# A 19-stage network on one core: the delta rule in 64-row blocks, weight splits placed anew, 512-column projection steps

## What is computed

```python
gc = jnp.cumsum(g, axis=-1)
decay = jnp.exp(jnp.where(causal, gc[..., :, None] - gc[..., None, :], -jnp.inf))
A = jnp.where(strict, jnp.einsum('bhncd,bhned->bhnce', k_beta, k) * decay, 0.0)
u = triangular_solve(eye + A, v * beta[..., None])
w = triangular_solve(eye + A, k_beta * jnp.exp(gc)[..., None])
attn_intra = jnp.where(causal, jnp.einsum('bhncd,bhned->bhnce', q, k) * decay, 0.0)
# for each of the four chunks in turn:
v_new = u_c - w_c @ state
o = qd @ state + a_c @ v_new
state = state * gl + kd.T @ v_new
```

## Time and profile before

| | |
|---|---|
| median of three runs | 3740.81 us (3738.6 to 3742.23) |
| the profiled execution's own time | 3740.95 us |
| its span in the profile | 3739.2 us |
| PE busy | 3435.3 us, 92% |
| DVE, ACT, POOL busy | 2060.6, 1559.5, 53.4 us |
| mean granted clock of TensorE | 0.943 |

### The profile page before, as it was taken

How to read it: one execution, slowest core, us unless ns; L and a number is a source line. 1 busy time by engine, 2 the same in 40 slices (tenths; PEclk the granted TensorE clock), 3 DMA queues, 4 the chain that set the end, 5 groups by cost and what they waited for, 6 DMA issues and landing times.

```text
span 3739.2 us, 48611 instructions
## 1 busy us (share of the span) xinstructions
PE 3435.3 (92%) x18972; PEld 2979.5 (80%) x18972; DVE 2060.6 (55%) x2413; ACT 1559.5 (42%) x1797; POOL 53.4 (1%) x84
## 2 busy tenths in 40 slices
PE   8986998998999999879999999999689999998899
PEld 6885887887887889768888888888668888887787
DVE  4557555545545567565554655555665455665554
ACT  4446444444444455114444444444344444531243
POOL 0000000000000020000000000000000000000000
PEclk9997998999999999789999999999889999988899
DMA  6542454454355554004555445555304555430154
GB/s 209 187 112 60 145 191 152 146 184 161 107 186 167 186 170 150 10 1 155 185 177 191 164 160 188 175 190 161 126 1 155 186 176 190 149 113 1 35 181 145
DMA packets 441172, 535.36 MB, mean 143 GB/s; under 512 B 21122, under 2 KB 405614, under 8 KB 441040
## 3 DMA queue, kind: packets, MB, share of 16 engines
q1 hardware_dynamic: 439248, 528.76, 44.1%
q0 software_dynamic: 1792, 4.72, 0.5%
HBM read 532.36 MB, written 1.05 MB: 143 GB/s over the span
## 4 chain that ended last, share of the span: by engine, by line
PE 86%; DVE 9%; ACT 3%; issue 1%; DMA 0%; SPq 0%; ACTq 0%; DVEq 0%
PE bank L132 22%; PE bank L134 22%; PE bank L133 22%; PE bank L129 3%; PE bank L130 3%; PE bank L131 3%; PE bank L309 2%; DVE w_lo L113 1%; PE bank L244 1%; ACT w_hi L105 1%; PE bank L1551 1%; PE bank L1558 1%; PE bank L1500 1%; PE bank L1581 1%; DVE arena L1750 1%
## 5 line engine op out<-in xcount | busy, mean ns | idle before, releaser
L113 DVE TENSOR_TENSOR w_lo<-raw,w_hi 128x2048 fp32r<-128x2048 f32 x514 | 1176.4, 2291 | 704.9 <-ACT w_hi L105 704.9
L105 ACT ACTIVATE w_hi<-raw 128x2048 fp32r<-128x2048 f32 x514 | 982.7, 1914 | 641.2 <-PE bank L134 527.4
L132 PE MATMUL bank<-w_hi,xT_hi 128*128 128x512 f32 (+3 forms) x3008 | 1101.9, 366 | 76.2 <-issue 33.2
L134 PE MATMUL bank<-w_hi,xT_lo 128*128 128x512 f32 (+3 forms) x3008 | 1088.4, 362 | 0.0
L133 PE MATMUL bank<-w_lo,xT_hi 128*128 128x512 f32 (+3 forms) x3008 | 1086.3, 361 | 0.0
L132 PEld LDWEIGHTS bank<-w_hi,xT_hi 128*128 128x128 f32 (+1 forms) x3008 | 580.0, 193 | 160.4 <-issue 43.5
L134 PEld LDWEIGHTS bank<-w_hi,xT_lo 128*128 128x128 f32 (+1 forms) x3008 | 578.7, 192 | 85.3
L133 PEld LDWEIGHTS bank<-w_lo,xT_hi 128*128 128x128 f32 (+1 forms) x3008 | 580.3, 193 | 79.8
L132 PE MATMUL bank<-w_hi,hidT_hi 128*128 128x512 f32 x1056 | 412.0, 390 | 0.0
L134 PE MATMUL bank<-w_hi,hidT_lo 128*128 128x512 f32 x1056 | 411.0, 389 | 0.0
L133 PE MATMUL bank<-w_lo,hidT_hi 128*128 128x512 f32 x1056 | 410.9, 389 | 0.0
(11 more groups left out here) (397 smaller groups left out, 2744.8 us busy)
## 6 DMA issues: line engine op xcount, KB each, us to landing
raw<-ffn_w_gate_up SPq DMA_DIRECT2D x352, 512.0 KB
raw<-ffn_w_down SPq DMA_DIRECT2D x264, 512.0 KB
raw<-ffn_w_gate SPq DMA_DIRECT2D x88, 512.0 KB
raw<-ffn_w_up SPq DMA_DIRECT2D x88, 512.0 KB
raw<-gdn_w_in SPq DMA_DIRECT2D x64, 512.0 KB
raw<-sc_w_in SPq DMA_DIRECT2D x24, 512.0 KB
raw<-rg_w_in SPq DMA_DIRECT2D x32, 336.0 KB
raw<-nsa_w_in SPq DMA_DIRECT2D x20, 512.0 KB
```

What stands on the lines that cost most here:

```text
L105: c.nc.scalar.activation(c.w_hi[r][:], c.raw[r][:], ACT.Copy).then_inc(c.sem("w_hi_split"), 1)
L113: c.nc.vector.tensor_tensor(c.w_lo[r][:], c.raw[r][:], c.w_hi[r][:].bitcast(F32), ALU.subtract).then_inc(c.sem("w_lo_split"), 1)
L132: mm(out, x_hi, w_hi, start=start, stop=False)
L134: return mm(out, x_lo, w_hi, start=False, stop=stop)
```

## The change

Three edits:

- **Delta rule.** Both chunks of a tile are kept in a 128 x 64 block, one chunk in rows 0 to 63, the other in rows 64 to 127, and all 16 pairs of head and tile (32 blocks of 64 x 64) go through together, in two groups of 8 (four heads, both tiles). Products are 64 x 64 x 64, ordered so that chunks, and thus row and column halves of the array, alternate (`quads`). q and k aren't scaled; the factors go into the small scalars. Preparation stands between gate steps. Masking of levels 2 to 5, the scalings of v and k and the gate's product move to POOL. In the recurrence the first chunk needs no state. ACT scales the state and reads `q state`. The output norm alternates between ACT, DVE and POOL.
- **Splits.** At the end of an FFN the split of slab b+3 moves ahead of the last hidden copy, and that of slab b+4 moves behind the next stage's norm (`late_slabs`: two slabs there instead of one, also after a stage whose last step has two slabs).
- **512-column steps.** Six groups of "tok" projections (the value half of w_kv, attn_w_o, sc_w_out, nsa_w_in, nsa_w_out, gdn_w_out twice) use steps of 512 columns, two slabs and two banks: 34 steps become 17.

```diff
+    for n in st.late_slabs:
+        dve_split(c, dve, slab_number(n, 0))
...
         hidden(f0 + j)
+        dve_split(c, dve, slab_number(b + 3, j))
         if last:
             last_hidden_lo(f0 + j)
-        dve_split(c, dve, slab_number(b + 3, j))
-        dve_split(c, dve, slab_number(b + 4, j))
+        else:
+            dve_split(c, dve, slab_number(b + 4, j))
...
+    def wide(weights, col0, steps):
+        return P_(weights, col0, steps, "tok", width=512, slabs=2, two_banks=True)
...
+def quads():
+    for flip in range(2):
+        for h4 in range(4):
+            for ch in range(2):
+                yield ch ^ flip, ch, h4
...
+    def small_products(b, lo, pair, lhs, rhs):
+        for t, ch, h4 in quads():
+            z, r = 8 * b + 4 * t + h4, rows_of(ch)
+            last = mm(c.bank[2 * pair + t][r, lo + h4 * G_CHUNK:lo + (h4 + 1) * G_CHUNK], lhs(r, z), rhs(r, z),
                       start=True, stop=True)
+        return last
...
+    for m in range(1, len(LEVELS)):
+        Am = v.Am[(m - 1) % 2]
+        for b in range(2):
...
+                pe.wait_ge(c.sem("gdn_X"), 8 * u + 2 * (m - 2) + b + 1)
+                pe.wait_ge(c.sem("gdn_A_level"), 10 * u + 2 * (m - 2) + 2 * (m > 3) + b + 1)
+            small_products(b, 0, b, lambda r, z: Am[r, z, :], lambda r, z: v.X[r, z, :]).then_inc(c.sem("gdn_ax"), 1)
+        for b in range(2):
+            pe.wait_ge(c.sem("gdn_T"), 12 * u + 2 * m + b + 1)
+            small_products(b, 256, b, lambda r, z: v.T[r, z, :], lambda r, z: v.Y[r, z, :]).then_inc(c.sem("gdn_y"), 1)
+            if m < len(LEVELS) - 1:
+                small_products(b, 0, 2 + b, lambda r, z: v.Y[r, z, :], lambda r, z: v.T[r, z, :]
+                               ).then_inc(c.sem("gdn_x"), 1)
...
+    pool.wait_ge(c.sem("gdn_tokens_read"), 2 * u + 1)
+    for b in range(2):
+        vb = by_tile(group(v.vb, b))
+        g.tensor_tensor(out=vb, in0=vb, in1=spread(group_cols(v.norm[:, :, G_HEADS:], b), G_DIM), op=ALU.mult
+                        ).then_inc(c.sem("gdn_tokens_scaled"), 1)
...
+    def level(m):
+        for b in range(2):
...
+            g.tensor_tensor(out=group(v.Am[(m - 1) % 2], b), in0=group(v.AQ, b)[:, :, 1, :],
+                            in1=per_head(v.level[m], 8), op=ALU.mult).then_inc(c.sem("gdn_A_level"), 1)
+    level(2)
+    level(3)
+    for b in range(2):
+        attn = group(v.AQ, b)[:, :, 0, :]
+        g.tensor_tensor(out=attn, in0=attn, in1=per_head(v.inclusive, 8), op=ALU.mult).then_inc(c.sem("gdn_A_level"), 1)
+    level(4)
+    level(5)
...
+    decay_state(1)
+    from_state(0)
+    decay_state(2)
+    squares(0)
+    root(0)
+    from_state(1)
+    squares(1)
+    root(1)
...
+    new_state(0)
+    new_values(1)
+    new_state(1)
+    new_values(2)
+    outputs(0)
+    new_state(2)
+    mean_squares(0)
+    new_values(3)
+    gated(0)
+    outputs(1)
+    mean_squares(1)
+    gated(1)
```

More of the change, by code:

```diff
@@ L585, in one @@
                 pe.wait_ge(c.sem("w_lo_split"), n + 1)
[L586 removed]
+        kd = pr.kd
+        kt = kd * len(slabs)
         lo, hi = pr.cols
@@ L589, in one @@
         if pr.two_banks:
-            order = [(tile, k) for q in range(len(slabs)) for tile in range(tiles) for k in range(q * KD, (q + 1) * KD)]
+            order = [(tile, k) for q in range(len(slabs)) for tile in range(tiles) for k in range(q * kd, (q + 1) * kd)]
         else:
@@ L1468, in pool_gdn @@
+    for m in range(len(LEVELS)):
+        step(g.tensor_tensor(out=v.full[m], in0=v.full[m], in1=v.upper, op=ALU.mult))
+    step(g.tensor_scalar(v.full[0], v.full[0], -1.0, None, ALU.mult))
+    compact = [(v.level[m], v.full[m]) for m in range(6)] + [(v.inclusive, v.upper), (v.ident, c.ident[:])]
+    for dst, src in compact:
+        for ch in range(2):
+            rows = slice(G_CHUNK * ch, G_CHUNK * (ch + 1))
+            step(g.tensor_copy(dst[rows, :], src[rows, rows]))
     assert made[0] == GDN_MASK_STEPS
-GDN_MASK_STEPS = 3 * 7 + 1 + 5 + 1 + 1
@@ L1598, in pe_gdn @@
-    pe_to_operand(c, pe, st, c.mix_out, "gdn_out", 2 * u + 2)
+    pe_project(c, pe, gate, after=beside_gate)
+    pe.wait_ge(c.sem("gdn_tokens_read"), 2 * u + 2)
+    for b in range(2):
+        for t in range(TOKS):
+            for h4 in range(4):
+                h = 4 * b + h4
+                for ch in range(2):
+                    tok = chunk_of(t, ch)
+                    last = mm(c.bank[4 + 2 * b + t][rows_of(ch), h4 * P:(h4 + 1) * P], v.cv[:, 8 + h, tok],
+                              v.cv[:, h:h + 9:8, tok], start=True, stop=True)
+            last.then_inc(c.sem("gdn_products"), 1)
@@ new lines, in pe_gdn @@
+    pe.wait_ge(c.sem("gdn_gaps"), 2 * u + 2)
+    pe.wait_ge(c.sem("gdn_kd_scale"), 2 * u + 2)
+    mm(c.bank[3][:, 0:2 * G_MATS], c.ones[0:G_MATS, :], flat(v.last), start=True, stop=True
+       ).then_inc(c.sem("gdn_products"), 1)
+    pe.wait_ge(c.sem("projection_read"), gate.step + gate.steps)
+    def small_products(b, lo, pair, lhs, rhs):
+        for t, ch, h4 in quads():
+            z, r = 8 * b + 4 * t + h4, rows_of(ch)
+            last = mm(c.bank[2 * pair + t][r, lo + h4 * G_CHUNK:lo + (h4 + 1) * G_CHUNK], lhs(r, z), rhs(r, z),
+                      start=True, stop=True)
+        return last
@@ new lines, in act_gdn, with decay_state @@
+    for b in range(2):
+        act.wait_ge(c.sem("gdn_uw"), 4 * u + b + 1)
+        if b == 0:
+            act.wait_ge(c.sem("gdn_y"), 10 * u + 10)
+        scalar.activation(flat(group(v.u, b)), c.pairs[b][:], ACT.Copy).then_inc(c.sem("gdn_u_read"), 1)
+    def decay_state(x):
+        act.wait_ge(c.sem("gdn_state"), 6 * u + 2 * (x - 1) + 2)
+        for h in range(G_HEADS):
+            n = x // 2 * G_HEADS + h
+            last = scalar.activation(v.decayed[:, h, :], v.state[:, h, :], ACT.Copy, scale=v.elast[:, x % 2, n:n + 1])
+        last.then_inc(c.sem("gdn_state_decayed"), 1)
```

724 lines of the change are left out of this document (398 added, 326 removed).

## The result

The changed kernel takes **3507.48 us** (median of 4 runs, 3506.62 to 3508.96) where the kernel before took 3739.7 beside it: ratio 0.938, interval 0.936 to 0.940, so 232 us less. The forecast was 3581, and even its range ended at 3530: right in sign, 74 us too slow. The profiled execution took 3508.96 with a span of 3507.0; before it was 3740.95 and 3739.2.

The account below looks back on a forecast made before the run. TensorE, busy 92% of the span, was taken as the bound, with the delta-rule parts a chain between PE, ACT and DVE. 3740.95 - 130 (delta rule) - 10.6 (512-column steps) - 19 (splits) = 3581 us; range 3530 to 3650.

Parts of the forecast that it names:

- The product: Delta rule: a 64 x 64 x 64 product costs 0.113 us, a record 0.054; an inversion level takes 10.9 us.
- u and w: Delta-rule phase after the inversion: 64 matmuls at 0.22 us, 14.4 us a part.
- The rival of full overlap: Weight loads of opposite quadrants run side by side: product 0.056 us, inversion 31 us, whole 3537; chance 0.18.
- The allowance of 9 us: Delta rule: given back in each part for stretches at half clock, leaving 65 us saved of 73.7.
- The sums of squares: Delta rule, with the gate steps: 32 matmuls at 0.22 us, 7 us as before.
- Recurrence: Delta-rule phase: 104 matmuls at 0.22 us, 23.3 us a part, with ACT's scaling of the state hidden.
- just fits: Delta rule: POOL's work plus DVE's blocking takes 38.9 of 39.5 us before level 2's use, so costed at nothing.
- Splits: Stage ends and starts: 25.1 us of waits for h saved, 5.5 us of stalls added, net 19 us less.
- The gross term: Stage ends: updating h as PE delivers saves 25.1 us of waits, before stalls are set against it.
- the stall: FFN starts: 0.55 us of wait for the moved split in ten FFNs, 5.5 us.
- 512-column steps: Tok projections: 34 steps in 195.8 us become 17 in 185.2 us, 10.6 us less.
- 0.22 a product, or slower: Two delta-rule rivals: product 0.22 us, whole 3683, chance 0.07; product of two whole record lengths, whole 4011, chance 0.04.

## Why the prediction was wrong, and where it was right

- **The product.** This is the step that failed. The prediction took 0.108 us a record from the earlier trace rows and wrote "halves of the rows don't share it, and the clock doesn't slow it". Sorting those very records makes them 0.176, so they share; and 64 x 64 records take 0.055 at clock 0.50 and 0.030 at 1.00, so the clock slows them. Row and clock were mixed: a row at the 1.2 GHz level, with overlap in it, was halved for half the columns and used for a stretch at 2.4 GHz. Its other support, 0.10 us a matmul from L1991, was read at clock 1.00, but its weights span all 128 rows, so no row halves alternate there: one support lacked the clock, the other the overlap. The 0.054 that came of the first is what a record costs with overlap at half clock. Its terms were 0.113 us for each of the 448 products from level 1 on and 0.22 for the 64 of u and w; they measured 0.061 and 0.116. That is 20 and 7 us a part, 54 of the 74 us.
- **The rival of full overlap** was right that opposite quadrants overlap: at full clock the recurrence's inner products gain a factor of 2.0, at half clock the inversion's gain at least 1.5 over eight in a row. The Trainium skill ("TensorEngine Tiling (Array Packing)", section Key Properties) says that different tiles load and multiply in parallel, and the trace agrees (0.059 us a record against 0.118); that should have weighed more than 0.18. Its numbers came out (a level of 6.3 us against 6.34, the inversion 31 against 30.9) partly by luck. It halved the forecast's price as one without overlap, but that price came from a row in which row halves overlapped already, and at half clock; the two mistakes nearly cancel. Its 3537 was still 30 too slow, since u and w overlapped too and the splits gave more.
- **u and w.** 0.22 for w's 128-column weights was taken over from the earlier trace rows with the same mistake: 64 moving columns and alternating row halves gave 0.118.
- **The allowance of 9 us** for half clock was about right: gate steps, preparation and tail are 7.3 over. The sums of squares, priced at 7 "as before", are its largest piece.
- **Recurrence**: 104 products at 0.22 held (23.3 against 22.5).
- **POOL** was never waited for, as forecast, with more room than "just fits": 1.9 us for 128 x 1024 (2.4 for the gate) and 1.27 for 128 x 512, against bounds of 3.7 and 1.85 from the earlier trace rows. The fit had been made from the upper bounds. The estimate of 2.3 us for 128 x 1024, half of the 4497 ns that the Trainium skill has for 2048 values ("GPSIMD Engine Reference", section Elementwise — side-by-side cycle accounting), was nearer to the measured 1.9. What was wrong is that DVE loses nothing.
- **Splits**: -19 forecast, -35 measured (-29 by the profiled spans). The sites were right. The gross term was 4 us too small, the stall 4 too large; why the first slab of an FFN waits so little stays open. The other 6 us are no term of the sum: the profiled execution was the slowest of its four, and no trace shows the median's.
- **512-column steps**: -10.6 forecast, about -9 measured, within the spread. The last step's second read wasn't wholly hidden: 0.5 us four times (waits of the transpositions for L714).
- **0.22 a product, or slower:** neither came. The run with sorted quadrants comes nearest to the first, with 0.168 a product and the clock at 0.50 as that rival had it; even then the kernel was 2.5% faster than before. What lets the clock rise there is the alternation.

## What to carry to other kernels

Small float32 matmuls on one part of the array should alternate with ones on another part, at least after each second product: it gains by overlap, and as much again or more by letting the granted clock rise (1.5 and 1.8 here). Never take a duration from a row without the clock of its stretch and the order of its neighbours beside it. A few microseconds saved ahead of a stage can be lost in it when its matmuls then begin in a half-clock stretch, so such edits must be timed whole and together.

## What the runs showed of the hardware that I had not expected

- Record of 64 x 64 weights and 64 moving columns: 0.030 us alternated at clock 1.00, 0.038 with four products in a row, 0.055 alternated at 0.50, 0.084 with eight in a row at 0.50. A PE busy for 75 us without a gap was granted half clock all along in that last case.
- The same weights with 128 moving columns: 0.059 us alternated and 0.118 in one quadrant at clock 1.00, 0.225 in one quadrant at 0.50. The same sequence of the recurrence ran at either level, by where the clock stood when it began.
- The clock fell in runs of full-array loads that move 16 columns or one (0.68 and 0.65 over them), and wide matmuls between them did not hold it up (0.50 for 23 us).
- Whether both quadrants write to one PSUM bank or to two makes no difference.
- GpSimd and VectorE hold each other up when both work in SBUF: 2.29 to 3.13 and 0.68 to 1.76 us on VectorE, 1.27 to 1.65 on GpSimd.
